# MLP of a hybrid decoder block in two phases, with the up product by one level of Strassen's method

## The chip, the cores and the metric

One Trainium2 chip, one core. The metric is the time of one execution on the device in microseconds; each kernel's figure is the median of its runs. The kernel works in float32: a product is made of three matmuls on float32r pieces (below), and the weights are read from HBM once.

## The reference, cut to what matters

One decoder layer on x (512 tokens, width 2048): a mixer sub-layer (projection, sparse attention, pooling mixer, recurrent branch, output projection) and then an MLP. Only the MLP changes:

```python
h = rms_norm(x, g_pre_mlp[l]) * (1.0 + scale2) + shift2
u = jax.nn.relu(h @ w_mlp_up[l])            # (512, 2048) @ (2048, 8192)
y = (u * u) @ w_mlp_down[l]                 # (512, 8192) @ (8192, 2048)
x = x + gate2 * rms_norm(y, g_post_mlp[l])
```

## The kernel before, in words

Each engine runs its own instruction stream, written by hand; semaphores join them. TensorE (PE) is fed by one chain: SyncE (SP) loads a slab of weights (128 partitions x 2 x 512) into `raw`, a ring of 4; ScalarE (ACT) rounds it to float32r, `w_hi` (L1356 in the MLP); VectorE (DVE) subtracts, `w_lo = raw - w_hi` (L1838). The function `three` (L731 to L733) makes a product of two such split operands: high by high, high by low, low by high, each matmul with its own load of the 128x128 stationary operand (PEld in the profile).

The mixer ends with the output projection. Its last part normalises x1 token tile by token tile (L1866 on DVE, the squares on ACT at L1114), makes a diagonal matrix of the inverse norms (L1569), and PE transposes and scales x1 with it (`turn_x1`, L780): 16 tiles of 128 features by 512 tokens. ACT (L1126) and DVE (L1574, L1576) turn each into h2_hi and h2_lo, and the first up matmuls follow feature tile by feature tile.

The MLP then goes in 8 steps of 1024 hidden channels (`mlp_step` on PE, `step` on DVE). In each, 2 up stages of 16 feature tiles x 4 hidden tiles give u; ACT takes relu, DVE squares and splits (L1902 to L1906); 4 down stages of 8 hidden tiles x 4 token tiles follow, and DVE adds each stage's 4 banks into `y2` in SBUF (L1921). Every matmul streams 512 columns: 8 x 2 x 16 x 4 x 3 = 3072 up, and 3072 down. GpSimd (POOL) has no part in the weights of the MLP; early in it, it computes the vector gate2 from 32 half slabs of w_mod (L712, L714, its own DMAs at L699), and PE sums that over partitions in the last step (L1049). The last stage runs token tile by token tile, each followed by its add, squares, gate, norm and store (L1969 to L1977).

Of the kernel before, what the change touches and what calls it, by code (L numbers as in the profile page):

```python
# [127 lines left out]
EARLY_SPLITS = RING + (KD - 4) // KS + 1  # L128
assert EARLY_SPLITS <= SG + 3
# [66 lines left out]
def build(nc, x, x_turned, columns_in, positions, pos_columns, w_mod_first, w_mod, w_in, w_key,  # L196
          pool_w, gate_r_w, gate_i_w, w_out, w_mlp_up, w_mlp_down, out):
# [15 lines left out]
    with ExitStack() as ctx:  # L213
# [61 lines left out]
        diag = at(150, "diag", [P, TT, P], F32)  # L275
# [70 lines left out]
        h2_hi = at(84, "h2_hi", [P, KD, T], F32R)  # L346
        h2_lo = at(116, "h2_lo", [P, KD, T], F32R)
        y2 = at(20, "y2", [P, TT, D], F32)
        u2_hi = at(52, "u2_hi", [P, HT, T], F32R)
        u2_lo = at(68, "u2_lo", [P, HT, T], F32R)  # L350
        u_relu = at(0, "u_relu", [P, 2, T], F32)
        u_sq = at(4, "u_sq", [P, 2, T], F32)
        g2_bc = at(12, "g2_bc", [P, D], F32)
        acc_g = at(12, "acc_g", [P, D], F32)
        gate_slabs = [at(kb, f"gate_slab{i}", [P, D // 2], F32) for i, kb in enumerate((8, 148))]
        x1_in = at(84, "x1_in", [P, TT, D], F32)
        junk2 = at(116, "junk2", [P, D], F32)
# [42 lines left out]
        x_again, x1_ready, x1_stored = [sem(f"x_again{t}") for t in range(TT)], sem("x1_ready"), [sem(f"x1_stored{t}") for t in range(TT)]  # L400
        y2_zero, y2_done, y2_squared = sem("y2_zero"), sem("y2_done"), sem("y2_squared")
        gate_landed, gate_step, gate_sum, gate_read = [sem(f"gate_landed{i}") for i in range(2)], sem("gate_step"), sem("gate_sum"), sem("gate_read")
        up_relu, up_used, u2_ready = sem("up_relu"), sem("up_used"), sem("u2_ready")
# [74 lines left out]
        def _(sp):  # L478
# [76 lines left out]
            def load_mlp(s, i, local):  # L555

                wait_count = MLP0 - PROJ_SLABS - RING + 1 + local
                sp.wait_ge(lo_dve, i * STEP_SLABS + wait_count)
                if local < UPG * SG:
                    g, j = divmod(local, SG)  # L560
                    src = w_up_d[:, KS * j:KS * j + KS, bass.ds(i * CHUNK + 512 * g, 512)]
                else:
                    g, j = divmod(local - UPG * SG, DS)
                    src = w_down_d[:, bass.ds(i * HT + KS * j, KS), 512 * g:512 * g + 512]
                sp.dma_start(raw[:, s % RING, :, :], src).then_inc(raw_landed[s % RING], 16)
# [3 lines left out]
            for local in range(STEP_SLABS):  # L569
                load_mlp(MLP0 + local, 0, local)  # L570
                if local == RING - 1:
                    for t in range(TT):
                        sp.wait_ge(x1_ready, t + 1)
                        sp.dma_start(x1_s[:, t, :], y1[:, t, :]).then_inc(x1_stored[t], 16)
            with sp.Fori(1, STEPS) as i:
                for local in range(STEP_SLABS):
                    load_mlp(MLP0 + local, i, local)
# [5 lines left out]
            for t in range(TT):  # L583
                sp.wait_ge(x1_stored[t], 16)
# [1444 lines left out]
```

## Time and profile before

| | us |
|---|---|
| median of 3 runs (2455.42 to 2466.59) | 2464.64 |
| the profiled execution, its own time | 2463.21 |
| its span, first to last instruction | 2461.4 |
| PE busy in the span | 2379.1 |
| DVE / ACT / POOL busy | 1224.5 / 681.9 / 573.8 |
| mean granted TensorE clock, share of full | 0.982 |

The span is the profiler's; the execution's own time is 1.8 us above it. Matmuls are pipelined, and the duration of one (some 0.4 us) is longer than the distance to the next; what one costs is the distance between starts. L numbers are lines of the kernel before.

### The profile page before, as it was taken

What the parts mean: (1) busy time and instruction counts of PE and PEld (TensorE: products, weight loads), DVE (VectorE), ACT (ScalarE), POOL (GpSimd) and SP (SyncE); (2) the same over time, 40 slices, a digit from 0 to 9 for tenths busy, and PEclk for the clock granted to TensorE, in tenths of its full rate; (3) what the DMA queues carried; (4) which work ended last, traced back from release to release, by engine and by line L of the source; (5) the groups of instructions that cost most, each with busy time, mean ns of one, the idle gap of its engine ahead of it and who ended that gap; (6) DMA issues with size and microseconds to landing.
All of it is one profiled execution on the core that took longest, in us unless ns stands there. A gap on an engine that the chain in (4) does not pass through costs nothing.

```text
span 2461.4 us, 27379 instructions
## 1 busy us (share of the span) xinstructions
PE 2379.1 (97%) x10724; PEld 1874.5 (76%) x10724; DVE 1224.5 (50%) x1570; ACT 681.9 (28%) x897; POOL 573.8 (23%) x345
## 2 busy tenths in 40 slices
PE   5999999999989998999999999999999999999997
PEld 1567878887767887888878888888888888888885
DVE  6649875991268664565353333333333333333336
ACT  4334434223255323321121221221221221221222
POOL 6535444444345000099920000000000000000000
PEclk8999999999999998999999999999999999999999
DMA  7967663332233584356533333333323323323224
GB/s 309 360 259 264 243 227 82 103 95 84 88 107 93 192 301 154 104 157 193 174 109 94 85 102 94 84 101 96 94 94 87 100 93 93 93 93 92 88 94 166
DMA packets 139488, 340.89 MB, mean 138 GB/s; under 512 B 15760, under 2 KB 17424, under 8 KB 127248
## 3 DMA queue, kind: packets, MB, share of 16 engines
q1 hardware_dynamic: 129744, 314.09, 38.8%
q0 software_dynamic: 4608, 16.78, 2.4%
q10 hardware_dynamic: 5056, 8.92, 1.0%
q8 instruction: 54, 0.88, 0.1%
q14 instruction: 26, 0.21, 0.0%
HBM read 322.70 MB, written 16.79 MB: 138 GB/s over the span
## 4 chain that ended last, share of the span: by engine, by line
PE 92%; DVE 4%; issue 1%; ACT 1%; DMA 1%; POOL 0%; DVEq 0%; ACTq 0%; PEldq 0%; POOLq 0%
PE psum L733 29%; PE psum L731 29%; PE psum L732 29%; PE psum L811 1%; PE psum L796 1%; PE psum L780 1%; ACT sq_out L1114 1%; DVE pt_lo L1795 0%; DMA mod_ring<-in_w_mod_first 0%; PE psum L773 0%; DVE probs L1782 0%; DVE x_in L1977 0%; DMA bias_s<-bias_out 0%; DMA pos_qi<-in_pos_columns 0%; DVE q_lo L1742 0%
## 5 line engine op out<-in xcount | busy, mean ns | idle before, releaser
L1838 DVE TENSOR_TENSOR w_lo<-raw,w_hi 128x1024 fp32r<-128x1024 f32 x256 | 331.2, 1301 | 713.2 <-ACT w_hi L1356 712.7
L731 PE MATMUL psum<-h_hi,w_hi 128*128 128x512 f32 (+1 forms) x1616 | 644.4, 399 | 7.2 <-issue 4.0
L732 PE MATMUL psum<-h_lo,w_hi 128*128 128x512 f32 (+1 forms) x1616 | 643.0, 398 | 0.0
L733 PE MATMUL psum<-h_hi,w_lo 128*128 128x512 f32 (+1 forms) x1616 | 642.8, 398 | 0.0
L1356 ACT ACTIVATE w_hi<-raw 128x1024 fp32r<-128x1024 f32 x256 | 270.9, 1060 | 1008.3 <-PE psum L733 1005.5
L733 PE MATMUL psum<-w_hi,u_lo 128*128 128x512 f32 x1024 | 407.4, 398 | 0.0
L731 PE MATMUL psum<-w_hi,u_hi 128*128 128x512 f32 x1024 | 403.1, 394 | 0.0
L732 PE MATMUL psum<-w_lo,u_hi 128*128 128x512 f32 x1024 | 403.1, 394 | 0.0
L731 PEld LDWEIGHTS psum<-h_hi,w_hi 128*128 128x128 f32 (+1 forms) x1616 | 305.3, 189 | 86.0 <-issue 10.8
L733 PEld LDWEIGHTS psum<-h_hi,w_lo 128*128 128x128 f32 (+1 forms) x1616 | 305.2, 189 | 75.3
L732 PEld LDWEIGHTS psum<-h_lo,w_hi 128*128 128x128 f32 (+1 forms) x1616 | 305.3, 189 | 74.0
L646 POOL TENSOR_TENSOR w_lo<-raw,w_hi 128x1024 fp32r<-128x1024 f32 (+1 forms) x96 | 255.8, 2669 | 342.7 <-ACT w_hi L1107 342.7
L732 PEld LDWEIGHTS psum<-w_lo,u_hi 128*128 128x128 f32 x1024 | 192.2, 188 | 49.0
L731 PEld LDWEIGHTS psum<-w_hi,u_hi 128*128 128x128 f32 x1024 | 192.2, 188 | 45.7 <-DVE w_lo L1838 0.2
L733 PEld LDWEIGHTS psum<-w_hi,u_lo 128*128 128x128 f32 x1024 | 192.2, 188 | 45.5
L1107 ACT ACTIVATE w_hi<-raw 128x1024 fp32r<-128x1024 f32 (+1 forms) x128 | 129.1, 1013 | 351.3 <-PE psum L733 317.3
L1921 DVE TENSOR_TENSOR y<-y,psum 128x512 f32<-128x512 f32 x112 | 69.4, 682 | 91.5 <-PE psum L733 91.5
L733 PE MATMUL psum<-w_hi,m_lo 128*128 128x512 f32 x256 | 102.9, 402 | 0.0
L732 PE MATMUL psum<-w_lo,m_hi 128*128 128x512 f32 x256 | 101.8, 398 | 0.0
L731 PE MATMUL psum<-w_hi,m_hi 128*128 128x512 f32 x256 | 101.8, 398 | 0.0
L712 POOL TENSOR_SCALAR gate_slab<-gate_slab,c_act 128x1024 f32<-128x1024 f32 x30 | 89.9, 2997 | 1.3
L714 POOL TENSOR_TENSOR acc_g<-acc_g,gate_slab 128x1024 f32<-128x1024 f32 x30 | 76.0, 2532 | 2.5
(268 smaller groups left out, 2200.8 us busy)
## 6 DMA issues: line engine op xcount, KB each, us to landing
raw<-in_w_mlp_up SPq DMA_DIRECT2D x128, 512.0 KB, 3.7
raw<-in_w_mlp_down SPq DMA_DIRECT2D x128, 512.0 KB, 3.8
raw<-in_w_in SPq DMA_DIRECT2D x88, 512.0 KB, 3.8
mod_ring<-in_w_mod_first SPq DMA_DIRECT2D x32, 1024.0 KB, 9.5
mod_slab<-in_w_mod SPq DMA_DIRECT2D x32, 1024.0 KB, 5.7
raw<-in_w_out SPq DMA_DIRECT2D x32, 512.0 KB, 5.8
slab<-in_w_mod SPq DMA_DIRECT2D x16, 1024.0 KB, 4.9
gate_slab<-in_w_mod POOLq DMA_DIRECT2D x32, 512.0 KB, 4.1
```

What stands on the lines that cost most here:

```text
L646: nc.gpsimd.tensor_tensor(w_lo[:, s % RING, :, 0:n], raw[:, s % RING, :, 0:n], w_hi[:, s % RING, :, 0:n].bitcast(F32), ALU.subtract).then_ ...
L712: ch.link(nc.gpsimd.tensor_scalar(gate_slabs[q % 2][:], gate_slabs[q % 2][:], c_act[:, k:k + 1], None, ALU.mult))
L714: nc.gpsimd.tensor_tensor(acc, acc, gate_slabs[q % 2][:], ALU.add).then_inc(gate_step, 1)
L731: nc.tensor.matmul(o, a_hi, b_hi, start=first, stop=False)
L732: nc.tensor.matmul(o, a_hi, b_lo, start=False, stop=False)
L733: return nc.tensor.matmul(o, a_lo, b_hi, start=False, stop=last)
L780: last = nc.tensor.matmul(o[:, P * t:P * t + P], src[:, t, P * kt:P * kt + P], diag[:, t, :], start=True, stop=True)
L796: last = nc.tensor.matmul(o[32 * j:32 * j + 32, :], blk_part[:, part, :], steps[:, k % STEP_SLOTS, :], start=part == 0, stop=part == 2)
L1107: nc.scalar.activation(hi, r, ACT.Copy).then_inc(hi_ready, 1)
L1356: nc.scalar.activation(w_hi[:, local % RING, :, :], raw[:, local % RING, :, :], ACT.Copy).then_inc(hi_ready, 1)
L1838: V.tensor_tensor(w_lo[:, local % RING, :, :], raw[:, local % RING, :, :], w_hi[:, local % RING, :, :].bitcast(F32), ALU.subtract).then_in ...
L1921: last = V.tensor_tensor(y, y, bank(n0 + UPG + d, t), ALU.add)
```

## The change

The whole MLP is rewritten; what precedes it stays, but for line numbers and the place of one buffer (`diag`).

**Up product.** Tokens, features and the 256 hidden channels of a unit are each cut in halves, so the product of a unit is a 2x2 by 2x2 product of quadrants. Winograd's form of Strassen's method makes it with 7 products of quadrants (OPS) in place of 8. It needs 4 sums of weight quadrants for every unit (S1 to S4, on POOL), 4 sums of activation quadrants once (T1, T2 on DVE, T3, T4 on POOL, each in two halves), and 7 sums of results for every unit (`comb`, on DVE, from PSUM): 15 kinds of sums. There are 32 units. A product is 8 feature tiles x 3 matmuls that stream 256 columns (the tokens of a half). The weights are laid out for this on the host (`w_up_units`).

**Squares.** ACT takes relu and square of a unit (128x1024 each, in `finish_unit`) and stores them to HBM (`u2_s`, 512 KB a unit).

**Down product.** It follows as a second phase, in two passes over 64 hidden tiles: one pass for 1024 of the 2048 output columns. For each hidden tile SP loads the weights (128x1024) and the squares (`uin`, 128x512); ACT and DVE split both; PE makes 4 token tiles x 2 halves x 3 matmuls of 512 columns into all 8 banks, which accumulate over the whole pass. Each pass ends token tile by token tile (`down_end`); between the passes the gate's sums, the squares of the banks (ACT) and their copies to `y2` (DVE) come. The gate's work on POOL starts after the last up product, and SP stores the finished gate (`store_gate`), waits for it and reads it back before it issues the loads of the last 4 hidden tiles.

**Handover.** ACT writes the 16 tiles of normalised x1 from PSUM to SBUF (`h_full_of`), then `b_high` (ACT) and `b_low` (DVE) split the operands of the 7 products, in 14 pieces of 128x1024, with `t_sum` (DVE) and the T3 and T4 of POOL between them.

```diff
+            def weight_sums(n, i):
...
+                    pool.wait_ge(op_lo, ops - 1)
+                nc.gpsimd.tensor_tensor(s_tmp[0][:], a21, a22, ALU.add).then_inc(s_ready, 1)
...
+                pool.wait_ge(s_ready, at_ + 1)
+                nc.gpsimd.tensor_tensor(s_tmp[1][:], s_tmp[0][:], a11, ALU.subtract).then_inc(s_ready, 1)
+                pool.wait_ge(s_ready, at_ + 2)
+                nc.gpsimd.tensor_tensor(a21, a11, a21, ALU.subtract).then_inc(s_ready, 1)
...
+            def last_sum(n, i):
+
+                wait_quads(pool, n, i, (Q12,))
+                pool.wait_ge(op_lo, i * (BLOCK * OPS) + (OPS * n + 2))
+                nc.gpsimd.tensor_tensor(s_tmp[0][:], unit_quad(n, Q12), s_tmp[1][:], ALU.subtract).then_inc(s_ready, 1)
...
+            def product(n, m, i, after=lambda k: None):
...
+                p = OPS * n + m
+                slot = p % RING
...
+                pe.wait_ge(op_lo, i * (BLOCK * OPS) + p + 1)
...
+                if not startup and m > 0:
+                    pe.wait_ge(comb_ready, combs + (COMB_OF[m] - N_COMBS))
+                o = op_bank(m)
+                for k in range(HALF):
+                    if startup and k % (HALF // 2) == 0:
+                        pe.wait_ge(b_lo_ready, 2 * m + k // (HALF // 2) + 1)
+                    a, c = divmod(P * k, 512)
+                    last = three(o, w_hi[:, slot, a, c:c + P], w_lo[:, slot, a, c:c + P], b_hi[OP_B[m]][:, k, :],
+                                 b_lo[OP_B[m]][:, k, :], k == 0, k == HALF - 1)
+                    if k == HALF - 1:
...
+            def op_high(n, m, i):
+
+                p = OPS * n + m
+                name = OP_A[m]
+                if name[0] == "S":
+                    act.wait_ge(s_ready, i * (BLOCK * N_SUMS) + (N_SUMS * n + int(name[1])))
...
+                    act.wait_ge(op_used, i * (BLOCK * OPS) + (p - RING + 1))
+                nc.scalar.activation(w_hi[:, p % RING, :, :], op_source(n, m), ACT.Copy).then_inc(op_hi, 1)
...
+            def op_low(n, m, i):
+                p = OPS * n + m
+                dve.wait_ge(op_hi, i * (BLOCK * OPS) + p + 1)
+                V.tensor_tensor(w_lo[:, p % RING, :, :], op_source(n, m), w_hi[:, p % RING, :, :].bitcast(F32),
+                                ALU.subtract).then_inc(op_lo, 1)
...
+            def comb(n, m, i):
...
+                dve.wait_ge(op_used, i * (BLOCK * OPS) + (OPS * n + m + 1))
+                if m == 2:
...
+                    V.tensor_tensor(u2_t[:], op_bank(2), p1_t[:], ALU.add).then_inc(comb_ready, 1)
+                    dve.wait_ge(comb_ready, at_ + 1)
+                    V.tensor_tensor(u4_t[:], op_bank(1), u2_t[:], ALU.add).then_inc(comb_ready, 1)
...
+            def load_group(i, cols, base):
+
+                for j in range(DN_GROUP):
+                    sp.wait_ge(down_lo, i * DN_GROUP + (base + j - RING + 1))
+                    load_down(j, i, cols)
+                    sp.wait_ge(uin_lo_ready, i * DN_GROUP + (base + j - RING + 1))
+                    load_v(j, i)
```

How the change moves the work, by the order of instructions on two engines.

DVE at the handover to the MLP, before: `h_full` and `h_lo` are the normalised x1 and its low part, in pieces of 512 columns.

```order
L1569 TENSOR_SCALAR diag<-ident,stat 128x128 x4
L1838 TENSOR_TENSOR w_lo<-raw,w_hi 128x1024 x2
L1574 TENSOR_SCALAR h_full<-psum,mul,mod 128x512
L1576 TENSOR_TENSOR h_lo<-h_full,h_hi 128x512
L1574 TENSOR_SCALAR h_full<-psum,mul,mod 128x512
```

DVE at the same place after the change, with that kernel's line numbers: `B_lo` and `T_lo` are low parts of the operands of products 0 to 6, L2209 and L2214 are the sums T1 and T2 (made in place in `h_raw`), L2143 is `op_low`, L2226 to L2240 are the combinations.

```order
L1873 TENSOR_SCALAR diag<-ident,stat 128x128 x4
L2143 TENSOR_TENSOR w_lo<-s_tmp,w_hi 128x1024 x2
L2143 TENSOR_TENSOR w_lo<-raw,w_hi 128x1024
L2202 TENSOR_TENSOR B_lo<-h_raw,B_hi 128x1024
L2209 TENSOR_TENSOR h_raw<-h_raw 128x1024
L2202 TENSOR_TENSOR T_lo<-h_raw,T_hi 128x1024
L2214 TENSOR_TENSOR h_raw<-h_raw 128x1024
L2143 TENSOR_TENSOR w_lo<-raw,w_hi 128x1024
L2202 TENSOR_TENSOR T_lo<-h_raw,T_hi 128x1024 x2
L2143 TENSOR_TENSOR w_lo<-s_tmp,w_hi 128x1024
L2202 TENSOR_TENSOR B_lo<-h_raw,B_hi 128x1024 x2
```

The operands of the activations are now made whole, in 14 pieces of 1024 columns with sums between them, where the first matmuls used to follow tile by tile.

POOL from the end of the attention on, before (`y` is y2, cleared for the adds).

```order
L671 TENSOR_TENSOR attn_sq<-attn 128x512 x3
L691 MEMSET y 128x4x512
L699 DMA gate_slab<-in_w_mod 128x1024 x2
L710 TENSOR_SCALAR acc_g<-gate_slab,c_act 128x1024
```

POOL at the same place after the change: L811, L814, L816 and L822 are S1 to S4 of a unit, L829 is T3, L836 is T4.

```order
L783 TENSOR_TENSOR attn_sq<-attn 128x512 x3
L811 TENSOR_TENSOR s_tmp<-raw 128x1024
L814 TENSOR_TENSOR s_tmp<-s_tmp,raw 128x1024
L816 TENSOR_TENSOR raw<-raw 128x1024
L829 TENSOR_TENSOR h_raw<-h_raw 128x1024 x2
L822 TENSOR_TENSOR s_tmp<-raw,s_tmp 128x1024
L836 TENSOR_TENSOR h_raw<-h_raw 128x1024 x2
L811 TENSOR_TENSOR s_tmp<-unit_odd 128x1024
```

POOL comes into the chain that feeds PE: 4 additions of two SBUF operands for every unit, the first three while x1 is still being normalised.

## Rows read from the trace of the kernel before

**Rows 1.** The page: the span and engines' busy time; the chain of waits.

```profile
span 2461.4 us, 27379 instructions
PE 2379.1 (97%) x10724; PEld 1874.5 (76%) x10724; DVE 1224.5 (50%) x1570; ACT 681.9 (28%) x897; POOL 573.8 (23%) x345
...
PE 92%; DVE 4%; issue 1%; ACT 1%; DMA 1%; POOL 0%; DVEq 0%; ACTq 0%; PEldq 0%; POOLq 0%
```

**Rows 2.** Busy time by stretch: handover, MLP start, its middle, the gate's matmuls.

```profile
978.00:992.00 14.00, 5.98 (x29) 6.01 (x30) 12.35 (x24) 9.46 (x12) 0.00 (x0) 0.51 0.72 253
992.00:1040.00 48.00, 48.00 (x260) 40.85 (x259) 27.37 (x34) 16.12 (x20) 2.97 (x3) 1.00 0.22 60
1300.00:2300.00 1000.00, 1000.00 (x4279) 804.25 (x4278) 340.95 (x390) 211.56 (x218) 0.00 (x0) 1.00 0.31 94
2306.00:2313.00 7.00, 7.00 (x40) 6.18 (x40) 3.48 (x8) 2.32 (x5) 0.00 (x0) 0.76 0.00 1
```

**Rows 3.** Timeline of PE in an up stage (start, duration, ...): 16 intervals between these.

```profile
1799.81 0.39 PE L733 MATMUL psum<-h_hi,w_lo 128*128 128x512 f32 x1
...
1803.56 0.40 PE L731 MATMUL psum<-h_hi,w_hi 128*128 128x512 f32 x1
```

**Rows 4.** The same in a down stage: 16 intervals between these.

```profile
1099.79 0.39 PE L733 MATMUL psum<-w_hi,u_lo 128*128 128x512 f32 x1
...
1103.52 0.40 PE L731 MATMUL psum<-w_hi,u_hi 128*128 128x512 f32 x1
```

**Rows 5.** Timeline of PE: 256-column matmuls of the attention, 10 intervals between these.

```profile
711.48 0.28 PE L732 MATMUL psum<-pt_lo,v_hi 128*128 128x256 f32 x1
...
712.68 0.28 PE L733 MATMUL psum<-pt_hi,v_lo 128*128 128x256 f32 x1
```

**Rows 6.** Timeline of PE: one-column matmuls of the gate, and the one behind them.

```profile
2305.69 3.63 PE L1049 MATMUL psum<-ones,acc_g 128*128 128x1 f32 x32
2309.18 0.67 PE L731 MATMUL psum<-h_hi,w_hi 128*128 128x512 f32 x1
```

**Rows 7.** Queries of single lines: duration min/median/max in ns.

```profile
L714 POOL TENSOR_TENSOR acc_g<-acc_g,gate_slab x30: 2397/2408/3472, 1055.9 to 1244.7; 128x1024 f32<-128x1024 f32 x30
L1838 DVE TENSOR_TENSOR w_lo<-raw,w_hi x256: 1211/1225/3433, 981.2 to 2425.8; 128x1024 fp32r<-128x1024 f32 x128
L1795 DVE TENSOR_TENSOR pt_lo<-psum,pt_hi x32: 674/679/692, 707.6 to 783.8; 128x512 fp32r<-128x512 f32 x32
L1552 DVE TENSOR_TENSOR mod<-mod,col x1: 2279/2279/2279, 343.8 to 343.8; 128x16 f32<-128x16 f32 x1
```

**Rows 8.** Timelines of POOL and DVE around 1116 us.

```profile
1116.52 2.40 POOL L714 TENSOR_TENSOR acc_g<-acc_g,gate_slab 128x1024 f32<-128x1024 f32 x1
...
1118.10 1.91 DVE L1838 TENSOR_TENSOR w_lo<-raw,w_hi 128x1024 fp32r<-128x1024 f32 x1
```

**Rows 9.** Timelines of PE, DVE and ACT at the handover to the MLP.

```profile
975.69 0.40 PE L733 MATMUL psum<-w_hi,m_lo 128*128 128x512 f32 x1
...
978.96 2.35 DVE L1866 SCALAR_TENSOR_TENSOR y<-y,stat,x_in 128x2048 f32<-128x2048 f32 x1
985.00 0.88 DVE L1569 TENSOR_SCALAR diag<-ident,stat 128x128 f32<-128x128 f32 x4
998.27 1.06 ACT L1356 ACTIVATE w_hi<-raw 128x1024 fp32r<-128x1024 f32 x1 [4.89 <-PE psum L733]
999.24 1.54 ACT L1126 ACTIVATE h_hi<-psum,mod,mul 128x512 fp32r<-128x512 f32 x2
```

**Rows 10.** DMA issues: KB each, median us to landing.

```profile
raw<-in_w_mlp_down SPq DMA_DIRECT2D x128, 512.0 KB, 3.8
gate_s<-mod SPq DMA_DIRECT2D x2, 8.0 KB, 12.4
```

**Rows 11.** Timelines of PE and DVE at the end: the last instruction of each.

```profile
2445.16 0.40 PE L733 MATMUL psum<-w_hi,u_lo 128*128 128x512 f32 x1
2455.79 2.48 DVE L1977 SCALAR_TENSOR_TENSOR x_in<-y,stat,x_in 128x1024 f32<-128x1024 f32 x2
```

More of the change, by code:

```diff
@@ L567, in _ @@
             wait_stage(sp, "mod4")
             sp.dma_start(x_in[3][:], x_d[:, 3, :]).then_inc(x_again[3], 16)
[L569 to L577, printed above, removed]
+            for qd in range(QUADS):
+                sp.wait_ge(lo_dve, OUT_SLABS - RING + qd + 1)
+                load_quad(0, qd)
@@ L693, in load_gate @@
+            with pool.Fori(1, UNITS // BLOCK) as i:
+                for n in range(BLOCK):
+                    weight_sums(n, i)
+                    last_sum(n, i)
+            pool.wait_ge(op_used, N_OPS)
             def load_gate(q):
@@ new lines, in _, with turn_beside @@
+            pe.wait_ge(diag_ready, TT)
+            for kt in range(HALF + HALF // 2):
+                turn_x1(kt)
+            def turn_beside(k):
+                if k < HALF // 2:
+                    turn_x1(HALF + HALF // 2 + k)
+            product(0, 0, 0, after=turn_beside)
+            for m in range(1, OPS):
+                product(0, m, 0)
+            for n in range(1, BLOCK):
+                for m in range(OPS):
+                    product(n, m, 0)
+            with pe.Fori(1, UNITS // BLOCK) as i:
+                for n in range(BLOCK):
+                    for m in range(OPS):
+                        product(n, m, i)
@@ new lines, in _ @@
+            for j in range(DN_GROUP):
+                down_ready(0, j)
+                for t in ((2, 3, 0, 1), (0, 1, 2, 3))[TURN_HALF]:
+                    if j == 0:
+                        pe.wait_ge(comb_ready, N_COMBS * UNITS - {2 * TURN_HALF: 1, 2 * TURN_HALF + 1: 0}.get(t, 2))
+                    for half in range(2):
+                        last = down(j, t, half, j == 0, False)
+                last.then_inc(down_used, 1)
+            with pe.Fori(1, UK // DN_GROUP - 1) as i:
+                down_group(i)
@@ new lines, in _ @@
+            down_end(UK // DN_GROUP - 1)
+            pe.wait_ge(y2_squared, 2)
+            pe.wait_ge(y2_done, 2)
+            pe.wait_ge(gate_step, 2 * KD)
+            for k in range(KD):
+                last = nc.tensor.matmul(down_bank(0, 0)[:, k:k + 1], acc_g[:, P * k:P * k + P], ones[:, 0:1], start=True, stop=True)
+            last.then_inc(gate_sum, 1)
+            for j in range(DN_GROUP):
+                down_ready(UK // DN_GROUP, j)
+                for t in (1, 2, 3, 0):
+                    if j == 0:
+                        pe.wait_ge(y2_squared, 2 * t + 2)
+                        pe.wait_ge(y2_done, 2 * t + 2)
+                    if j == 0 and t == 0:
+                        pe.wait_ge(gate_read, 1)
+                    for half in range(2):
+                        last = down(j, t, half, j == 0, False)
+                last.then_inc(down_used, 1)
@@ new lines, in after_product @@
+            def after_product(n, m, i, last=False):
+                if m >= 2:
+                    comb(n, m, i)
+                p = OPS * n + m + RING
+                if last and p >= BLOCK * OPS:
+                    down_low(0, p - BLOCK * OPS, True)
+                else:
+                    op_low(p // OPS, p % OPS, i)
+            for hf in range(2):
+                b_low(0, hf)
+                t_sum("T1", hf)
+            for hf in range(2):
+                b_low(1, hf)
+                t_sum("T2", hf)
```

640 lines of the change are left out of this document (413 added, 227 removed).

## Prediction, made before the changed kernel was run

> **What bounds the kernel now.** I read the page first: PE is busy 2379.1 of 2461.4 us and holds 92% of the chain of waits [rows 1]. The busy time by stretch shows the same in the MLP: from 1300 to 2300 us PE is busy all of the time at full clock, DVE a third, ACT a fifth, and DMA 31% [rows 2]. So the time of the MLP is the number of matmuls times the distance between two starts, and that I took from the timeline of PE: 16 intervals in 3.75 us up, 0.2344 each [rows 3], and in 3.73 us down, 0.2331 each [rows 4]. Only a few stretches are not PE's. At the handover PE's last matmul of the output projection starts at 975.7 and the diagonal matrix that lets it transpose is made from 985.0 [rows 9]; there the clock is 0.51 of full [rows 2]. At the end DVE works 13 us beyond PE [rows 11].
>
> **The change, part by part**
>
> *Up matmuls.* 3072 of 512 columns go (at 0.2344: 720.1 us). 32 x 7 x 8 x 3 = 5376 of 256 columns come, each with a full load of stationary weights. The question is whether such a load hides behind half the columns. The attention has this very shape: 10 intervals in 1.20 us, 0.120 [rows 5], and 5 neighbouring bursts that I read give 0.119. One-column matmuls with the same load stand 3.63/32 = 0.113 apart at the most [rows 6]: that is the floor of the load, and 256 columns lie just above it. I take 0.1195, so a product costs 24 x 0.1195 = 2.87 us and a unit 20.07. Bounds: half of 0.2344, 0.1172, and 0.125, for waits at the product's edges that the bursts of 12 don't show (the waits at the slabs of before cost nothing in rows 3 and 4). By count the saving is 720.1 - 642.4 = 77.7 us.
>
> The Trainium skill (TensorE: Matmul & The Clock Gate, Back-to-back issue gap) gives 262 cycles at 256 columns, 109 ns. By it the 5376 would cost 587 us, 56 less; for 512 columns it gives 216 ns where rows 3 show 234, so the row of the same shape decides.
>
> *Down matmuls.* Still 3072 of 512 columns at 0.2331: 716.1 us. The 32 one-column matmuls of the gate (3.6 us [rows 6]) and the slow clock behind them (0.24 of 7 us, 1.7 [rows 2]) move from the last step to the seam of the passes, at the same price. The last bank's squares and copy lie beside them. For both seams I allow 2 us (0 to 5).
>
> *What feeds a product.* For each: one ACT rounding of 1.06 us [rows 9], one DVE subtraction of 1.22 [rows 7], and for 4 of 7 a POOL sum, which I price by POOL's addition of the same shape, 2.41 [rows 7]. What matters most here is this: the DVE subtraction that starts at 1118.10 takes 1.91 us, and ends 1.1 us after the POOL addition does (1118.92) [rows 8]. DVE and POOL operations with two inputs in SBUF exclude each other. The DVE sums with one input in PSUM (L1795) never rise over 0.69 [rows 7], so the combinations stand outside. A unit thus needs 4 x 2.41 + 7 x 1.22 = 18.2 us of the shared path in 20.07 of PE: enough, with 9% to spare. The ring of 4 lets a rounding start when the product 4 before has ended, 3 products (8.6 us) ahead of need; the worst turn is 1.06 + 2.41 + 1.22 = 4.7. POOL's S1 of the next unit waits for the low part of S4 of this one; from there S1 to S3, each losing one turn to DVE, take 3 x 3.6 = 11 us and S4 3.6 more, of 20. DVE's own time is 8.5 + 7 combinations of about 0.41 (an estimate: 0.68 for 512 columns and 1.22 for 1024 give 0.41 for 256) = 11.4. ACT has 7 x 1.06 + 0.4 + 2 x 1.06 = 10. So in the steady part I cost all of this at nothing; PE covers it.
>
> *Handover, the cost.* Before, PE starts up matmuls at 992.3 and is full from there on [rows 2]. After:
> 1. POOL's S1 to S3 of unit 0 start when the projection ends, at 976.1, and hold the shared path until 983.4. DVE's normalisation of the last token tile (978.96, two SBUF inputs [rows 9]) loses to them. Its small two-input operations can wait as well: one of 16 columns (L1552) took 2.28 us [rows 7]. It ends up to 4.5 us later; I take 4 (0 to 4.7).
> 2. From the 4th transposed tile (992.6), ACT has 13 tiles at 0.82 (half of 1.54 [rows 9] and its own wait) and 4 roundings of 1.06: 16 tiles ready at 1007.5.
> 3. Behind that stand, to the last operand of product 6, 18 DVE operations (2 of T2, 11 low parts, 5 `op_low`) and 9 of POOL (T3, T4, S4 of unit 0, S1 to S4 of unit 1) in mutual exclusion: 18 x 1.22 + 9 x 2.41 = 43.7, and 2 for combinations. To 1053.2, then half a product, 1.4: 1054.6.
> 4. With the 4 of point 1, and 1.4 for products at half clock after waits: 1060 as the end of unit 0. If nothing excluded anything, the DVE operations alone would give 1033; at most I see 1066.
>
> PE does 20 us of products in these 68. This is what the change pays.
>
> *End.* DVE's adds of `y2` go. Per token tile it has 2 gate products (0.69 each), a small chain of 1.2, 2.5 for the last operation and some 0.2 of waits, 5.3 in all, against 5.6 of PE; it starts after 8 earlier gate products. I get 9.3 us from PE's end to DVE's end, where it was 12.9 (2445.4 to 2458.3 [rows 11]), and 3.1 for the last store as now: 12.4.
>
> *Transfers.* The down phase loads 768 KB for each hidden tile of 24 x 0.2331 = 5.6 us, 140 GB/s, more than the 94 of now [rows 2]; a 512 KB load lands in 3.8 [rows 10], and loads overlap. It is issued some 19 us ahead. The gate's store takes 12.4 us to land [rows 10], and the last 4 tiles' loads queue behind it on SP: 19 - 12.4 leaves 6.6 for a landing of 3.8. Free, but the thinnest cover of all; without it PE would wait some us once.
>
> *Sum.* 1060 + 31 x 20.07 (622.2) + 716.1 + 3.6 + 1.7 + 2 + 12.4 = 2418.0 of span. With 1.8 around it the profiled execution would take 2419.8, against 2463.2; the median of before is 1.4 above its profiled execution, so 2421.
>
> **Rivals**
> - *The handover costs less* (exclusion milder, normalisation not delayed): unit 0 ends near 1035, 2396. For it: many overlapped DVE operations of before kept their 1.22 (the median in rows 7). Against: those lay beside POOL's one-input operations. 0.14.
> - *DVE and POOL set the pace.* If DVE waits through each POOL sum with its combinations queued behind, nothing overlaps: 9.6 + 8.5 + 2.9 = 21.1 a unit, 31 x 1.0 more, 2453. 0.09.
> - *They do, and the clock falls with them: slower.* If PE runs dry once a unit and its clock drops to half, as it did behind the wait at 978 to 992 [rows 2], each drop costs the 1.7 us seen at 2309: 22.8 a unit, 31 x 2.7 = 85 more, 2506. The change turns slower when a unit passes 21.9 us. For it: 9% to spare, and in-order engines. Against: the ring's 8.6 us, and combinations that can run beside POOL. 0.16, which includes a late load in the down phase. The Trainium skill (SBUF — State Buffer, Who interferes with whom) says that only a DVE instruction with two SBUF inputs contends with POOL's reads, which speaks against the full 21.1 and so against both of these.
> - *Long runs of 256 columns reach the floor of the load*, 0.113 [rows 6]: 5208 x 0.0065 = 34 less, 2387. The bursts in rows 5 are all near 0.120. 0.03. The Trainium skill's 109 ns (the section named above) would make it 2366.
> - *The saving by count doesn't come*, 0.13 or more per matmul: 5376 x 0.0105 = 56 more, 2477, just slower. 0.03.
>
> **How the numbers follow.** The forecast has 0.55, its own range 2402 to 2440 from the bounds above. A measurement of this kernel tells about 0.5%, 12 us, from no change: faster is under 2452, slower over 2477. Faster: 0.55 + 0.14 + 0.03 and half of the 2453 case, 0.76. Same: the rest of it and the near side of the last two, 0.07. Slower: 0.17. The range leaves out the floor's case and most of the slow one: 2392 to 2470.
>
> **What would show it.** In the profile after: 256-column matmuls 0.119 to 0.120 apart, 24 a product, with no gap at its edges; the second unit starts near 1060; POOL sums at 2.4 to 3.6 and `op_low` with a tail up to 3.6; full clock from there. PE idle before product 5 of each unit (the one on S4) and clock digits below 9 would make the slow rival right; an end of unit 0 before 1040 the first one. A span of the up phase above 690 us or of the down phase above 730 would make me wrong.

## The result, and the profile after

| | before | after |
|---|---|---|
| median of 4 runs each | 2462.22 | 2400.48 |
| lowest and highest | 2455.42, 2466.59 | 2396.48, 2407.57 |
| the profiled execution, its own time | 2463.21 | 2396.48 |
| its span | 2461.4 | 2394.7 |

The change is faster: ratio 0.9762, 95% interval 0.9743 to 0.978. The forecast was 2421 against 2464.64: the sign and the mechanism hold, and the saving between the medians is 61.7 us where 43.6 were forecast. The page of the changed kernel, span, busy time and chain of waits, against [rows 1]:

```profile
span 2394.7 us, 33923 instructions
PE 2288.4 (96%) x13028; PEld 1928.3 (81%) x13028; DVE 1530.2 (64%) x1692; ACT 900.5 (38%) x1167; POOL 953.8 (40%) x476
...
PE 91%; DVE 5%; ACT 1%; issue 1%; DMA 1%; POOL 0%; DVEq 0%; ACTq 0%; SPq 0%; PEldq 0%; POOLq 0%
```

PE is still the bound. 90.7 us of its busy time are gone, and 66.7 us of the span. The busy time by stretch of the changed kernel, against [rows 2] (span and stretch; PE, PEld, DVE, ACT, POOL; granted clock, DMA share, GB/s). The stretches are the end of the mixer, the handover, the up units, the first pass down, the seam, the second pass:

```profile
968.00:990.00 22.00, 7.89 (x50) 7.48 (x49) 14.89 (x24) 12.72 (x17) 7.03 (x3) 0.69 0.39 143
990.00:1050.00 60.00, 36.65 (x255) 35.12 (x254) 47.81 (x31) 28.79 (x34) 26.64 (x9) 0.83 0.14 53
1100.00:1640.00 540.00, 540.00 (x4605) 540.00 (x4604) 482.65 (x384) 265.49 (x273) 313.72 (x111) 1.00 0.36 134
1665.00:2010.00 345.00, 345.00 (x1480) 277.54 (x1479) 147.08 (x124) 97.66 (x128) 196.88 (x92) 1.00 0.63 206
2018.00:2030.00 12.00, 11.70 (x54) 10.12 (x53) 6.83 (x11) 4.40 (x9) 0.00 (x0) 0.72 0.79 264
2030.00:2380.00 350.00, 350.00 (x1502) 281.58 (x1501) 123.25 (x150) 98.79 (x132) 0.00 (x0) 1.00 0.42 132
```

In the up phase DVE is busy 482.65 of 540 us, where it had been at a third, and yet PE never stops and its clock is whole. 540 us hold 4605 matmuls: 0.1173 each. The timeline of PE shows one product of 24 between the first and the next one's first matmul, 2.82 us, and the step over the edge costs nothing:

```profile
1198.87 0.28 PE L884 MATMUL psum<-T_hi,w_hi 128*128 128x256 f32 x1
...
1201.69 0.28 PE L884 MATMUL psum<-B_hi,w_hi 128*128 128x256 f32 x1
```

The waits of the changed kernel from 1100 to 1600 us (engine and line, whom it waited for: us in total, times, longest) have no wait of PE among the long ones, but two that tell how near the feeders are. POOL waits 7 us a unit for DVE's low part of S4, because S1 overwrites what that reads:

```profile
ACT w_hi L1563 <- PE psum L886: 191.7, 128, 1.8
POOL s_tmp L811 <- DVE w_lo L2143: 183.0, 26, 7.5
DVE w_lo L2143 <- ACT w_hi L1563: 51.4, 25, 2.5
```

DVE and POOL in one unit (timelines of both; start, duration):

```profile
1201.03 3.10 DVE L2143 TENSOR_TENSOR w_lo<-unit_odd,w_hi 128x1024 fp32r<-128x1024 f32 x1
1207.73 3.31 DVE L2143 TENSOR_TENSOR w_lo<-s_tmp,w_hi 128x1024 fp32r<-128x1024 f32 x1
1211.30 2.34 DVE L2143 TENSOR_TENSOR w_lo<-unit_odd,w_hi 128x1024 fp32r<-128x1024 f32 x2
```
```profile
1199.78 3.27 POOL L814 TENSOR_TENSOR s_tmp<-s_tmp,unit_odd 128x1024 f32<-128x1024 f32 x1
1203.13 3.26 POOL L816 TENSOR_TENSOR unit_odd<-unit_odd 128x1024 f32<-128x1024 f32 x1
1207.56 2.41 POOL L822 TENSOR_TENSOR s_tmp<-unit_odd,s_tmp 128x1024 f32<-128x1024 f32 x1 [1.17 <-DVE w_lo L2143]
```

The exclusion of [rows 8] is there in every pair: a subtraction of 1.22 us shows as 2.3 to 3.3 when a POOL sum is open. But the durations contain waiting that overlaps with the other engine's work, so they must not be added. What adds is the distance: S2 to S3 is 3.35 us with one subtraction in it, and two subtractions back to back take 2.34 together, so the second adds 1.14. A subtraction thus costs the shared path 1.14 and a POOL sum 3.35 - 1.14 = 2.21.

**Where the 66.7 us of span came from.** P below is the start of the last matmul of the output projection. It lies in work that the change doesn't touch, at 975.69 before [rows 9] and 968.14 after; in the traces of all the kernels that follow it lies between 967.7 and 977.9. What happens in the MLP is therefore measured from P.

| part | forecast | measured after |
|---|---|---|
| P (unchanged work) | 975.7 | 968.1 |
| P to the first matmul of unit 1 | 84.3 | 81.5 |
| 31 units | 622.2 | 611.1 |
| down matmuls, gate, both seams | 723.4 | 723.9 |
| last matmul to the end | 12.4 | 10.1 |
| span | 2418.0 | 2394.7 |

Of the 23.3 us that the span falls short of the forecast, 11.1 are the spacing of the matmuls, 7.6 the earlier P, which is no effect of the change, 2.8 the handover, 2.3 the tail, and the down part gives back 0.5.

Against the kernel before, from P to the end: 1485.7 us have become 1426.5, 59.2 less. The up matmuls save 720.1 - 5376 x 0.1173 = 89.5, and the end is 6.1 shorter (16.2 from the last matmul's start, [rows 11], now 10.1). So 36.4 of 95.6 us went at the handover and the seams.

### The profile page after: what moved, and what is told of

Same layout as the page of the kernel before. It is cut to its first block, busy times and chain, and to the rows that moved or that the text cites. A ratio compares the mean times of both kernels' runs of the same rounds, so it can differ in the third digit from the quotient of the medians.

```text
span 2394.7 us, 33923 instructions
## 1 busy us (share of the span) xinstructions
PE 2288.4 (96%) x13028; PEld 1928.3 (81%) x13028; DVE 1530.2 (64%) x1692; ACT 900.5 (38%) x1167; POOL 953.8 (40%) x476
## 4 chain that ended last, share of the span: by engine, by line
PE 91%; DVE 5%; ACT 1%; issue 1%; DMA 1%; POOL 0%; DVEq 0%; ACTq 0%; SPq 0%; PEldq 0%; POOLq 0%
PE psum L884 29%; PE psum L886 29%; PE psum L885 29%; PE psum L949 1%; PE psum L964 1%; DVE steps L1807 1%; DVE pt_lo L2099 1%; DVE probs L2086 0%; PE psum L926 0%; DVE T_lo L2202 0%; ACT h_raw L1611 0%; DVE B_lo L2202 0%; DVE q_lo L2046 0%; DMA pos_qi<-in_pos_columns 0%; DVE probs L2093 0%
## 5 line engine op out<-in xcount | busy, mean ns | idle before, releaser
L886 PE MATMUL psum<-w_hi,uin_lo 128*128 128x512 f32 x1024 | 406.5, 397 | 0.0
L884 PE MATMUL psum<-w_hi,uin_hi 128*128 128x512 f32 x1024 | 405.9, 396 | 0.0
L885 PE MATMUL psum<-w_lo,uin_hi 128*128 128x512 f32 x1024 | 403.0, 394 | 0.0
L884 PE MATMUL psum<-T_hi,w_hi 128*128 128x256 f32 x1024 | 288.9, 282 | 17.1 <-DVE T_lo L2202 17.1
L885 PE MATMUL psum<-T_lo,w_hi 128*128 128x256 f32 x1024 | 288.4, 282 | 0.0
L886 PE MATMUL psum<-T_hi,w_lo 128*128 128x256 f32 x1024 | 288.4, 282 | 0.0
L2143 DVE TENSOR_TENSOR w_lo<-s_tmp,w_hi 128x1024 fp32r<-128x1024 f32 x96 | 222.6, 2320 | 63.7 <-ACT w_hi L1563 63.7
L884 PE MATMUL psum<-h_hi,w_hi 128*128 128x512 f32 (+1 forms) x592 | 236.4, 399 | 6.7 <-issue 4.0
L886 PE MATMUL psum<-h_hi,w_lo 128*128 128x512 f32 (+1 forms) x592 | 235.9, 399 | 0.0
L885 PE MATMUL psum<-h_lo,w_hi 128*128 128x512 f32 (+1 forms) x592 | 235.7, 398 | 0.0
```

The costliest lines, as they stand in the source:

```text
L884: nc.tensor.matmul(o, a_hi, b_hi, start=first, stop=False)
L885: nc.tensor.matmul(o, a_hi, b_lo, start=False, stop=False)
L886: return nc.tensor.matmul(o, a_lo, b_hi, start=False, stop=last)
L2143: V.tensor_tensor(w_lo[:, p % RING, :, :], op_source(n, m), w_hi[:, p % RING, :, :].bitcast(F32), ALU.subtract).then_inc(op_lo, 1)
```

## The experiments

Times are one profiled execution each unless said otherwise. "Unit" is the distance between the same matmuls of neighbouring units, as the mean from unit 1 to the last.

| run | time | P to unit 1 | unit | distance without gaps, ns |
|---|---|---|---|---|
| the change | 2396.48 | 81.5 | 19.71 | 117.3 |
| e1, S1 and a half | 2400.06 | 82.8 | 19.71 | 117.3 |
| e2, S1 twice | 2403.9 | 83.4 | 19.71 | 117.3 |
| e9, S1 three times | 2470.07 | 88.7 | 21.60 | 118.2 |
| e3, an eighth product | 2495.12 | 84.7 | 22.53 | 117.3 |
| e4, two products halved | 2378.24 | 79.6 | 19.28 | 117.9 |
| e5, S4 before T3 | 2394.65 | 79.7 | 19.71 | 117.3 |
| e6, T3 and T4 on DVE | 2393.55 | 74.2 | 19.71 | 117.3 |
| e7, B22's split earlier | 2400.6 | 78.7 | 19.94 | 118.7 |
| e10, S1 to S3 after `diag` | 2406.7 | 81.2 | 19.94 | 118.7 |
| e8, e5 to e7 together | 2402.34 | 73.3 | 19.94 | 118.7 |
| e11, the change again | 2401.9 | 81.5 | 19.71 | 117.3 |
| e12, e5 to e7 again | 2394.25 | 73.6 | 19.71 | 117.3 |

### Does the path shared by DVE and POOL set the pace?

**e1: POOL makes half of S1 once more.**

```diff
+                nc.gpsimd.tensor_tensor(s_tmp[0][:, :, 0:256], a21[:, :, 0:256], a22[:, :, 0:256], ALU.add).then_inc(s_extra, 1)
+                pool.wait_ge(s_extra, i * BLOCK + n + 1)
                 nc.gpsimd.tensor_tensor(s_tmp[0][:], a21, a22, ALU.add).then_inc(s_ready, 1)
```

> POOL makes the first half of S1 once more in every unit (1.2 us of two-input POOL work, same result). Theory (PE sets the unit at 24 x 7 x 0.1173 = 19.7 us, and the path that DVE and POOL share in exclusion is needed for 4 x 2.41 + 7 x 1.22 = 18.2): 19.4 needed, so the unit stays at 19.7 and the span within 5 us of the change's 2394.7. Rival (the shared path already sets the pace, as the waits that lengthen op_low to 2.1 to 2.4 us suggest): 31 x 1.2 = 37 us more.

The unit stays at 19.712 us to the nanosecond shown, and no interval between two up matmuls of the steady part is above 0.3 us. That the shared path sets the pace is out. The span is 3.6 us longer, because P lies 4.0 later.

**e2: all of S1 twice.** The same edit with whole tiles.

> POOL makes all of S1 once more in every unit (2.41 us more). Theory (exclusion counts, PE sets the pace up to 19.7): 20.6 us needed on the shared path, so the unit grows to 20.6 or a little more and the span by 28 us or more, with PE waiting on op_low. Rival (only POOL's own chain counts, and POOL stands idle 7 us before each S1): nothing, the span within 5 us of 2394.7.

Again 19.712, and no wait of PE. The span is 7.4 us longer, more than the 5 that the rival allowed, but not in the units: 5.6 are P's and 1.9 lie between P and unit 1. The added sum went into POOL's idle time. Timeline of POOL in this kernel, with its own line numbers; L812 is the added sum, and the 7 us of idle time before S1 in the change are 4.01:

```profile
1204.79 2.40 POOL L812 TENSOR_TENSOR s_tmp<-unit_odd 128x1024 f32<-128x1024 f32 x1 [4.01 <-DVE w_lo L2146]
1207.27 3.28 POOL L814 TENSOR_TENSOR s_tmp<-unit_odd 128x1024 f32<-128x1024 f32 x1
1210.63 3.27 POOL L817 TENSOR_TENSOR s_tmp<-s_tmp,unit_odd 128x1024 f32<-128x1024 f32 x1
```

By durations, as the prediction added them, five sums and seven subtractions need 5 x 2.41 + 7 x 1.22 = 20.6 us and don't fit into 19.7. By distances they need 5 x 2.21 + 7 x 1.14 = 19.0, and do. The measurement sides with the distances. By them the change itself needs 4 x 2.21 + 8.0 = 16.8 of 19.7 us.

**e9: S1 three times.**

> POOL makes S1 three times in every unit (4.8 us more than the change, same result). With S1 twice the unit stayed at 19.71 us, though 4 + 1 additions of 2.41 and 7 subtractions of 1.22 make 20.6: in the trace an addition and a subtraction that exclude each other follow at 3.35 us a pair, not 3.63, and subtractions alone at 1.14. Revised theory (exclusion by these spacings): 6 x 2.21 + 7 x 1.14 = 21.2 us needed at the least, and by POOL's own chain 6 x 3.35 and the wait for S4's low part, 22 to 23: PE runs dry, the unit takes 21.2 to 23 us, the span grows by 46 to 100. Rival (extra sums go into POOL's idle time, 4 us of which are left in each unit): at most 1 us a unit, under 31 more.

By distances six sums need 6 x 2.21 + 8.0 = 21.2; the unit takes 21.60, and the one time of this kernel is 0.4% above the one before (2470.07 against a median of 2459.45 and a highest of 2463.19 in 9 runs on the same chip). The edge lies between one and two added sums. The busy time by stretch of e9 shows PE short of work for the first time, and the waits from 1100 to 1600 us name POOL as what ACT waits for:

```profile
1100.00:1700.00 600.00, 570.48 (x4646) 553.73 (x4645) 523.58 (x388) 263.60 (x276) 498.24 (x167) 1.00 0.32 122
```
```profile
ACT w_hi L1567 <- POOL s_tmp L815: 167.4, 23, 7.3
POOL s_tmp L813 <- DVE w_lo L2147: 79.2, 23, 3.5
...
PEld psum L888 <- DVE w_lo L2147: 28.4, 51, 0.9
PE psum L888 <- DVE w_lo L2147: 24.7, 69, 0.7
```

PE waits several times a unit, up to 0.9 us each, and the granted clock in the stretch stays 1.00. So the loss is the waiting alone. The slow rival of the prediction had put half clock on top of it; with waits this short no row shows that.

There is a second measure of the path, which needs no split into 2.21 and 1.14: the time in which at least one POOL sum or one DVE subtraction is open, counted from the starts and durations of the rows between 1100 and 1600 us. Of 500 us it is 438 in the change, 459 in e1, 488 in e2 and 496 in e9. So the path is full in e9, and the change leaves 12% of it free by this count, 15% by distances. What e9 doesn't tell apart is the path and POOL's own chain: POOL's sums (413.5 us) and its waits for the low part of S4 (79.2) fill the same 500 us nearly as well. The expectation priced that chain at 22 to 23 us, and the unit is 21.60.

### Is PE the bound, and by how much?

**e3: product 6 of each unit is made twice**, which takes Strassen's saving back: 8 products for 7, all other work unchanged.

```diff
-                for k in range(HALF):
+                for r, k in [(r, k) for r in range(2 if m == OPS - 1 else 1) for k in range(HALF)]:
```

> Product 6 of each unit is made twice by PE (24 matmuls of 256 columns more for each unit, same result), so that PE does the 8 products of a plain product of quadrants. Theory (PE sets the pace): 24 x 0.1173 = 2.82 us a unit, 31 to 32 x 2.82 = 87 to 90 more, span 2482 to 2485, slower than the kernel before. Rival (DVE and POOL set it): less than half of that.

The unit grows by 2.816 us, 24 x 117.3 ns, without a gap. Its span is 98.6 us longer than the change's: 31 x 2.816 = 87.3 in these units, 3.2 from P to unit 1, where the first of the added products lies, 9.8 for a later P, and 1.7 less in the down phase. At 2495.12 it is 34.6 slower than the kernel before in the same job, one run of each, and still 24.8 slower with the 9.8 of P taken off. So two things are shown: every matmul of the up phase is paid for in full, and without the eighth that Strassen's method saves, the two-phase form with its handover would be a loss.

**e4: products 5 and 6 use 4 of 8 feature tiles.** This leaves out half of two products, so the up product is incomplete. PE would need 144 x 0.1173 = 16.9 us a unit.

```diff
-                for k in range(HALF):
+                last_k = HALF // 2 - 1 if m >= 5 else HALF - 1
+                for k in range(HALF // 2 if m >= 5 else HALF):
```

> Products 5 and 6 of each unit are made from 4 of 8 feature tiles (this leaves out part of the up product), so PE needs 16.9 us a unit. What the unit then takes is what its feeding can do. Theory (exclusion on the shared path): 18.2 to 19.4 us a unit, 10 to 47 us less than 2394.7. Rival (feeding has much in hand, since its waits overlap): 16.9, 87 less.

The unit falls to 19.28 on average (19.35 to 19.5 once it has settled), not to 16.9. PE now waits up to 1.05 us at some products, though POOL still idles 6.7 us before each S1. The chain of e4, followed back from 1219 us (start, duration), shows what closes the loop:

```profile
1202.78 0.41 DVE u_t L2239
1203.19 1.02 DVE w_lo L2144
...
1206.34 0.42 DVE u_t L2241
1206.79 1.07 ACT u_t L1641
1207.88 1.07 ACT u_st L1647
1209.10 0.34 ACTq L1653
1209.63 1.07 ACT w_hi L1564
...
1212.66 2.86 DVE w_lo L2144
```

The first entry follows a product of PE that ran from 1199.64 to 1202.78. Then the orders written for DVE and ACT chain a subtraction that waits for POOL's S4, the last combination, relu, square and the store's issue of the finished unit, the rounding of the next S4, and subtractions up to the operand of the product that starts at 1219.00, one unit later: 19.36 us. It is in-order work of ACT and DVE with one product of PE in it, not the sum of anybody's busy time, and 2% below PE's 19.71. The reading is from this one trace; no run took a link of the loop out. What the run shows by itself is that fewer matmuls would have bought almost nothing: of 2.8 us a unit taken from PE, 0.4 came back. The span, 18.3 us less than the change's, lies in the range of the theory (10 to 47), but the reason given there, the length of the shared path, is not what this chain shows.

### What is the handover made of?

**e5: S4 of unit 0 goes before T3 on POOL** (`last_sum(0, 0)` moved up by one block).

> In the handover POOL makes S4 of unit 0 before T3 instead of behind it, in the time when POOL waits for the 16 tiles. From the last matmul of the output projection to the first of unit 1 the change takes 81.5 us. Theory (the handover lasts as long as its two-input operations of DVE and POOL take one after another): 2.4 to 3.4 less, 78 to 79. Rival (it lasts as long as the chain T4, loads of unit 1's quadrants into its memory, rounding on ACT that waits for them): 0 to 2 less.

**e6: T3 and T4 are made by DVE**, at their places in its order, and POOL's are dropped.

```diff
-                nc.gpsimd.tensor_tensor(h2_quad["T3"][:, k, :], h2_quad["B22"][:, k, :], h2_quad["B12"][:, k, :],
-                                        ALU.subtract).then_inc(t_pool, 1)
...
+                V.tensor_tensor(h2_quad[name][:, k, :], h2_quad[left][:, k, :], h2_quad[right][:, k, :],
+                                ALU.subtract).then_inc(t_pool, 1)
```

> T3 and T4 are made by DVE (1.22 each half) instead of POOL (2.41). Theory (sum of exclusive operations): 4 x 1.2 = 4.8 us less than 81.5. Rival (chain over T4 and the loads): T4 is complete some 3.4 us earlier, so 3 to 4 less.

e5 gains 1.7 us from P to unit 1, inside the rival's 0 to 2 and short of the theory's 2.4. e6 gains 7.3, more than either account gave; it contains e5's edit, since with T3 and T4 gone from POOL's order S4 of unit 0 stands directly behind S3. The rival names what was not in my prediction, a wait behind T4, and it stands in the timeline of POOL in the change. What it had wrong in e6 is how much earlier T4 would end: 3.4 us, where 7.4 were measured.

```profile
1021.07 5.69 POOL L836 TENSOR_TENSOR h_raw<-h_raw 128x1024 f32<-128x1024 f32 x2 [8.03 <-DVE B_lo L2202]
1031.61 2.37 POOL L811 TENSOR_TENSOR s_tmp<-unit_odd 128x1024 f32<-128x1024 f32 x1 [4.85 <-DMA unit_odd<-in_w_up_units]
```

In the code SP waits for both halves of T4 (`sp.wait_ge(t_pool, 4)`) before it loads the last two quadrants of unit 1, since these lie where x1 lay. T4 ends at 1026.76, the loads land by 1031.6, POOL idles 4.85 us and ACT 7.46, and only then come S1 to S4 of unit 1. So the end of T4 times the handover. Measured from P, with the T4 rows of each kernel:

| | end of T4 | first matmul of unit 1 | between |
|---|---|---|---|
| the change | 58.6 | 81.5 | 22.9 |
| e5 | 56.7 | 79.7 | 23.0 |
| e6 | 51.2 | 74.2 | 23.0 |
| e10 | 57.9 | 81.2 | 23.3 |
| e7 | 58.8 | 78.7 | 19.9 |

In e6 T4 is made in 2.36 us on DVE where POOL took 5.69, with the subtractions ahead of it free of the exclusion. Its row in the timeline of DVE in e6, where P is 972.9:

```profile
1021.77 2.36 DVE L2249 TENSOR_TENSOR h_raw<-h_raw 128x1024 f32<-128x1024 f32 x2
```

T4 ends 7.4 us earlier and unit 1 starts 7.3 earlier. e5, e6 and e10 move the end of T4 and leave the rest at 23 us; that settles e6, and it is the rival's chain.

**e7: the split of B22 (product 5) goes before the weights of product 4** on ACT and DVE.

```diff
-            for m in range(2, OPS):
-                for hf in range(2):
-                    b_high(m, hf)
+                for mm in ((m, m + 1) if m == 4 else (m,) if m != 5 else ()):
+                    for hf in range(2):
+                        b_high(mm, hf)
```

(the same for `b_low`)

> ACT and DVE split the operand of product 5 (B22) before, and not behind, the rounding of unit 1's A11, which waits for loads that land at 1031.6. No operation is added or taken away. Theory (sum of exclusive operations): 0 to 1 less than 81.5. Rival (what waits behind the loads in ACT's order): 3 to 5 less, and PE's wait before product 5 (6.2 us) nearly gone.

It is the one that shortens the second stretch, by 3 us: B22's operands no longer wait behind the late loads. The gain of 2.8 is a little under the rival's 3 to 5. PE's wait of 6.2 us before product 5 is gone as the rival has it, but most of it comes back before product 6, where PE waits 6.8 us instead of 1.7. The time is 2400.6, no better than the change's: in this execution the matmuls of the whole phase stood 118.7 ns apart, not 117.3, which costs 31 x 0.224 = 6.9 us.

**e10: POOL starts S1 to S3 of unit 0 only when `diag` is made** (`pool.wait_ge(diag_ready, TT)` ahead of them).

> POOL starts S1 to S3 of unit 0 only when the diagonal matrix is made. The change takes 13.5 us from the last projection matmul to the first diagonal operation, the kernel before 9.3. Theory (the sums hold up DVE's normalisation by exclusion): back to 9.3 to 9.5. But ACT's roundings of S1 and S2 stand ahead of its first tile, so the first tile leaves ACT at 16 to 17 us as in the change (16.7), and unit 1 starts within 2 us of the change's 81.5. Rival (something else delays the normalisation): 13.5 stays.

The normalisation of the last token tile in the change, against 2.35 us in [rows 9], and in e10 (timelines of DVE):

```profile
971.40 2.07 DVE L1755 TENSOR_TENSOR stat<-stat 128x1 f32<-128x1 f32 x1
973.50 4.51 DVE L2180 SCALAR_TENSOR_TENSOR y<-y,stat,x_in 128x2048 f32<-128x2048 f32 x1
...
981.63 0.88 DVE L1873 TENSOR_SCALAR diag<-ident,stat 128x128 f32<-128x128 f32 x4
```
```profile
976.34 0.16 DVE L1756 TENSOR_TENSOR stat<-stat 128x1 f32<-128x1 f32 x1
976.53 2.35 DVE L2181 SCALAR_TENSOR_TENSOR y<-y,stat,x_in 128x2048 f32<-128x2048 f32 x1
...
982.49 0.87 DVE L1874 TENSOR_SCALAR diag<-ident,stat 128x128 f32<-128x128 f32 x4
```

`diag` is begun 13.5 us after P in the change and 9.2 in e10 (9.3 before). The exclusion did cost the normalisation's chain 4.3 us, as the prediction had it: 2.2 in the operation on 2048 columns, and 1.9 in the small one ahead of it, which has a single column and took 2.07 us beside a POOL sum, 0.16 without. But unit 1 starts only 0.3 earlier, for in ACT's order the roundings of S1 and S2 stand ahead of the transposed tiles. ACT now waits for the later sums (timeline of ACT in e10), and starts the first tile 17.0 us after P, where it was 16.7:

```profile
985.89 1.06 ACT L1564 ACTIVATE w_hi<-s_tmp 128x1024 fp32r<-128x1024 f32 x1 [4.64 <-POOL s_tmp L811]
...
990.30 3.46 ACT L1612 ACTIVATE h_raw<-psum,mod,mul 128x512 f32<-128x512 f32 x4
```

The delay was real, and putting the sums behind it only exchanged it for another wait. What it would be worth with ACT's order changed too was not tried.

### The three edits of the handover together, and the spacing

**e8: e5, e6 and e7 together**, 5 runs timed.

> The three edits of the handover together. Sum theory: 7 to 8 less; both mechanisms: 9 to 13 less than 81.5. The span 2382 to 2387, and the ratio to the kernel before lower than the change's 0.976 by 0.003 to 0.005.

P to unit 1 falls to 73.3, a gain of 8.2. Both mechanisms together had given 9 to 13, and the single gains don't add: e6 alone, which contains e5, has 7.3 of it, and e7's edit, worth 2.8 by itself, adds 0.9. The split of B22 that it moved (timeline of DVE in e8) now lies beside S1 of unit 1 on POOL, from 1031.82, and takes 4.55 us, where in e7 it was over before the loads landed and took 2.35:

```profile
1030.72 4.55 DVE L2191 TENSOR_TENSOR B_lo<-h_raw,B_hi 128x1024 fp32r<-128x1024 f32 x2
```

The median is 2395.11, ratio to the kernel before 0.9741 (0.9727 to 0.9754), 0.002 below the change's where 0.003 to 0.005 were expected. The profiled execution took 2402.34, and its phase again stands at 118.7 ns. Since e7, e8 and e10 had 118.7 and the others 117.3, the question was whether the code sets it.

**e11 and e12: the change, and the code of e8, both once more, on one chip, 5 runs each.**

> The change itself, once more, on one chip with the next. In the traces so far the 256-column matmuls stand either 117.3 ns apart (5 kernels) or 118.7 (2 kernels, which differ from others only in the handover), for the whole phase. If chance at the phase's start decides, the spacing of this trace can be either, and the 5 times spread over 7 us; if the code decides, it is 117.3 again. Median 2398 to 2402.

> The three handover edits again, beside the change on the same chip: unit 1 starts 8 us earlier (73.3 after the projection), so the median is 4 to 9 us below that of the change. If chance decides the spacing, this trace can show 117.3 where the first showed 118.7.

The busy time by stretch of the same code in e8, then in e12:

```profile
1100.00:1640.00 540.00, 540.00 (x4553) 540.00 (x4552) 476.47 (x380) 263.74 (x271) 307.89 (x110) 1.00 0.35 131
```
```profile
1100.00:1640.00 540.00, 540.00 (x4605) 540.00 (x4604) 482.63 (x385) 265.03 (x273) 312.99 (x111) 1.00 0.36 135
```

4553 matmuls in 540 us are 118.6 ns each, 4605 are 117.3, at the same clock and without a gap in either. So the code alone does not set it. Nor does the chip alone: e5 to e8 ran on one and e9 to e12 on another, and both values stand on each. The same code was not traced twice on one chip. Each phase shows one of the two from its beginning to its end. What chooses stays open. The 6.9 us between the two would be enough for the spread of this code's runs (2393.97 to 2402.34), but only the profiled ones show their spacing, and P, which moves by 10 us between the traces, would be enough as well. The five runs of e11 lie within 1.3 us, not over 7 as the account by chance expected.

e11: median 2401.9, 0.9767 (0.9754 to 0.9781) of before. e12: median 2398.49, 0.9754 (0.9738 to 0.977). The 8 us of the handover show in the traces (81.5 against 73.6), but the medians are 3.4 apart, less than the 4 to 9 expected, and the intervals of the two ratios overlap. Over both jobs the code of e8 has a median of 2396.1 in 10 runs, and the change 2401.9 in 9, with its 4 first ones. That this code beats the change as a whole is likely and not shown; that both beat the kernel before is.

## Why the prediction was right, and where it was off

**The bound and the saving by count: right, the spacing mis-sized.** I took 0.1195 us from bursts of the attention [rows 5]; 5376 matmuls at 0.1173 are 11.8 us less, 11.1 of them after unit 0. The lower bound that I had written down, half of the 512-column distance, was the value: 0.2344 / 2 = 0.1172. The bursts of 12 were the wrong row to prefer. In the e-runs 118.7 appears too, and 0.1195 in no steady phase. The floor's case, 0.113, and the case of 0.13 or more are out.

**The rule of the Trainium skill** (TensorE: Matmul & The Clock Gate, Back-to-back issue gap), 109 ns at 256 columns, which the page gives for matmuls by themselves, is not borne out for this stream of matmuls with a load each: every phase without gaps, in eleven traces, shows 117.3 or 118.7.

**What feeds a product: right that it costs nothing, wrong in the sum.** "18.2 of 20.07, 9% to spare" added durations. By distances it is 16.8 of 19.71, 15% to spare (12% by the time in which the path is open), and e2 and e9 bracket the edge where that sum puts it. The combinations take 0.41 to 0.43 (the estimate was 0.41), and run beside POOL's sums. What I did not see is the chain of e4: ACT's work for a finished unit stands ahead of the next S4. By that one trace it leaves 2% where the busy times leave much more. Both rivals that let DVE and POOL set the pace needed a 21.1 us path; the measured one reaches that only with two more sums of POOL, and then, in e9, the time does pass that of before, at a unit of 21.60. The point that I gave for it, 21.9, which has 12 us of tolerance in it, was near; half clock had no part in it. The other rule that I cited (SBUF — State Buffer, Who interferes with whom) agrees: the PSUM combinations keep their length, the two-input SBUF operations don't.

**Handover: the size right, one mechanism missing.** 84.3 forecast, 81.5 measured. Point 1, the delay of the normalisation, is 4.3 us for 4 (e10). Point 2: the 16th tile has left ACT 35.9 us after P; 31.8, and 35.8 with point 1's delay, were forecast. Points 3 and 4 gave 43.7, 2, and twice 1.4 from there, 48.5, nearly all of it mutual exclusion. The distance is 45.6, and 4.85 of them are POOL's wait for loads that SP issues after T4. I had read the sums of POOL in their order, but not past which queue T4 stands: what is queued behind it is SP. Too much exclusion, by adding durations, and a missing wait made up for each other: that the total came within 3 us was luck. That a sum has the right size proves none of its terms; it took e6 to see it.

**Down, seams: right.** The rows of the seam (timeline of PE in the change):

```profile
2018.87 0.40 PE L886 MATMUL psum<-w_hi,uin_lo 128*128 128x512 f32 x1
2019.57 5.49 PE L1277 MATMUL psum<-ones,acc_g 128*128 128x1 f32 x32 [0.30 <-PE psum L886]
2024.92 0.77 PE L884 MATMUL psum<-w_hi,uin_hi 128*128 128x512 f32 x1
2025.49 0.63 PE L885 MATMUL psum<-w_lo,uin_hi 128*128 128x512 f32 x1
```

The gate's 32 matmuls take 5.49 us, not the 3.63 of [rows 6]: the clock falls while they run (0.72 in the stretch), and the first ones of the second pass are slow as well. 3.6, 1.7 and 2 for both seams were forecast, 7.3 in all; it is 723.9 - 3071 x 0.2331 = 8.0, of which 0.6 are the matmuls of the passes at 0.2333, and the first seam has no gap. This execution is not the rule: in 7 of the 12 other traces the 32 matmuls ran before the clock fell, and the down part took 722.2. So it was in e1 (timeline of PE), with 0.86 over 12 us from 2022:

```profile
2024.82 3.70 PE L1280 MATMUL psum<-ones,acc_g 128*128 128x1 f32 x32 [0.30 <-PE psum L889]
```

The gate's store lands in 12.8 us (median of the kernel's two such stores), forecast 12.4, and no wait of PE follows: the thin cover held.

**Tail: mis-sized.** Forecast 12.4, measured 10.1. The last DVE operations in the change:

```profile
2385.82 0.69 DVE L2298 TENSOR_TENSOR y<-psum,g_bc 128x512 f32<-128x512 f32 x1 [0.26 <-ACT sq_end L1314]
...
2389.02 2.48 DVE L2316 SCALAR_TENSOR_TENSOR x_in<-y,stat,x_in 128x1024 f32<-128x1024 f32 x2
```

DVE ends 6.9 us after the last matmul's start at 2384.57, 6.7 after its end as the forecast counted, which had 9.3. I had it lag behind with gate products of earlier tiles; it has finished these, even waits 0.26 us, and has one tile's work left.

**The range** (2392 to 2470) held the time near its lower end; the forecast's own range (2402 to 2440) missed it by 1.5 us. By the number alone the first rival, with 2396, was nearer, but its mechanism was not there: it had unit 0 end near 1035, 59 us after P, and it ended after 81.5. 7.6 us of the miss in the profiled span are P's, which no step could give.

## What to carry to other kernels

Where two engines exclude each other, price an operation by the distance to the next start in a full stretch and not by its duration, which holds the other's share too; then find the order of in-order engines that closes a loop, since a bound engine without a single wait can have 2% or 15% to spare behind it, and only taking work from it (e4) and adding to its feeders (e2, e9) tells which. A change of algorithm pays for its operands at the phase's start: here, of 95.6 us gained in matmuls and tail, 36.4 went there for the most part, so look there for what is loaded behind the last use of a buffer. Fewer matmuls of half the size are priced by half of the measured distance of the large ones, as long as the one-column floor [rows 6] lies below.

## What the runs showed of the chip that I had not expected

- The distance of 256-column matmuls, each with a load, takes one of two values for a whole phase, 117.3 or 118.7 ns, in different executions of the same code (e8 and e12, on two chips), at full granted clock and without a gap. The 512-column matmuls of the second pass down stand 233.3 ns apart in all thirteen traces, whichever of the two the up phase shows.
- With waits of up to 0.9 us several times a unit (e9: PE busy 570.48 of 600 us) the granted clock stayed 1.00, while the 12 us at the seam, with 0.3 us of idle time and 32 one-column matmuls, show 0.72. The same stretch of instructions shows 0.86 in e1, where the clock fell only behind the 32.
- An added POOL sum of 2.4 us a unit, 77 us in all, cost a DVE-busy phase nothing after unit 0 (DVE 527.31 busy of 540 us in e2), though DVE and POOL exclude each other: busy time of DVE rose by 45 us without its work growing.
